# Six of the 42 low parts of each two-pass expert's weight tiles are made by GpSimd

## The chip, the cores and the metric

The kernel runs on one core of one Trainium2 chip. The metric is device time in microseconds (us) of one execution: 1571.8 us, the median of three runs (1571.66 to 1572.39). The engines are TensorE (PE; its weight loads are PEld), VectorE (DVE), ScalarE (ACT), GpSimd (POOL) and SyncE (SP), which issues the weight loads to the DMA engines.

## The reference

Two encoder layers over 256 tokens of width 1024, and a last RMSNorm. Layer 0 is a pooling mixer and a dense SwiGLU, layer 1 an attention mixer and a mixture of eight experts, of which each token takes two. The change lies in the experts:

```python
def _swiglu(h, w_gate_up, w_down):
    gu = h @ w_gate_up
    g, u = gu[..., :D_FF], gu[..., D_FF:]
    return (jax.nn.silu(g) * u) @ w_down

def _moe(h, router, w_gate_up, w_down):
    logits = (h @ router).astype(jnp.float32)
    top_v, top_i = lax.top_k(logits, TOP_K)
    gates = jax.nn.softmax(top_v, axis=-1)
    ...
    y = jnp.zeros_like(h)
    for e in range(N_EXPERTS):
        y = y + gate_full[..., e:e + 1] * _swiglu(h, w_gate_up[e], w_down[e])
    return y
```

D_FF is 3584. All weights are float32.

## The kernel before

**Numbers in two parts.** TensorE multiplies in a rounded float32 format. A weight tile (128 partitions x 2048, 1 MB) is therefore split into a high part, `whi` (ScalarE copies it into that format, `make_hi`, L314), and a low part, `wlo` = raw - high (VectorE subtracts, `make_lo`, L320). The tokens are split in the same way. A three-pass product adds high x high, high x low and low x high, 12 matmuls of 512 columns for a tile.

**Experts.** The experts are put in an order by how many tokens they have, and worked one after the other as items n = 0 to 7 (item n is also called expert n below). Each has 42 tiles: 28 of gate and up weights, in seven slabs of four (two gate tiles, which are summed in bank G, two up tiles in bank U), then 14 down tiles (banks Y0, Y1). Items with even n have up to 128 tokens and three passes (`full_item`). Items with odd n have up to 64 tokens, and the two parts of the tokens lie side by side in the 128 columns of TensorE, so that two passes do: 8 matmuls for a tile (`half_item`, L902, L903 in the gate stage, L939, L940 in the down stage). After each slab TensorE adds the two halves again with 16 small matmuls into bank T (`turn_slab`, L915), ScalarE and VectorE take the SiLU, the product `th` (L1768) and split it into `hTh` (ScalarE, and a small low part by VectorE, L1350).

**Rings and waits.** SP loads tile t into one of seven raw buffers (RAW = 7); the load of tile t waits until the low part of tile t-7 is made. `whi` and `wlo` have three buffers (CUT = 3): both parts of tile t wait until TensorE has used tile t-3 (`tile_used`). TensorE waits for the low part of a tile, which implies its high part. Every engine works its own written order, so one that waits holds up all that is behind it on that engine.

**GpSimd in the experts.** For each item it issues a gather of the next item's tokens (`e_tok`, L488), when their row numbers are there (`from_ready`, made by VectorE after slab 6 has begun), and at the item's end one or two scatter-adds of its result (L496). Before the last norm the sum is read back (L501).

Of the kernel before, what the change touches and what calls it, by code (L numbers as in the profile page):

```python
# [28 lines left out]
P = 128  # L29
RAW = 7  # L30
CUT = 3
# [10 lines left out]
E = 8  # L42
CAP = 128
HALF_CAP = 64
LOW = 4
# [6 lines left out]
ALU = mybir.AluOpType  # L52
ACT = mybir.ActivationFunctionType
F32 = mybir.dt.float32
# [11 lines left out]
FFN_TILES = DOWN + 2 * DT  # L66
T_ATT = T_FFN + FFN_TILES
HALF_TILES = 20
T_MOE = T_ATT + 2 * HALF_TILES
# [4 lines left out]
def count(i, per, plus=0):  # L74

    if isinstance(i, int):
        return i * per + plus
    register, step, first = i
    return register * (step * per) + (first * per + plus)


def one(i):
# [7 lines left out]
def encoder(nc, x_in, rel_bias, gains_t, norm_ffn, norm_final, a_w_in, a_w_group, a_scale, a_w_out,  # L90
            b_w_in, b_w_out, f_w_gate_up, f_w_down, m_router, m_w_gate_up, m_w_down,
            c_ident, c_pool, c_bucket, c_band, c_class, c_tri, c_iota, c_tab, c_dump, out):
    with ExitStack() as ctx:
        sem = lambda name: ctx.enter_context(nc.semaphore(name))
# [17 lines left out]
        raw = place("raw", [RAW, 2048], F32)  # L112
# [114 lines left out]
        spare_zero = sem("spare_zero")  # L227
        c_in = [sem(f"const{i}") for i in range(15)]
        raw_full = [sem(f"raw_full{i}") for i in range(RAW)]
        hi_done, lo_done, tile_used = sem("hi_done"), sem("lo_done"), sem("tile_used")  # L230
        chain = sem("chain")
        ms_done, std_done, hn_done = sem("ms_done"), sem("std_done"), sem("hn_done")
        rstd_done, x_sum, sq_done = sem("rstd_done"), sem("x_sum"), sem("sq_done")
# [76 lines left out]
        def make_hi(act, t, item=0):  # L310
# [2 lines left out]
                act.wait_ge(tile_used, count(item, FFN_TILES, t - CUT + 1))  # L313
            nc.scalar.activation(whi[:, t % CUT], raw[:, t % RAW], ACT.Copy).then_inc(hi_done, 1)  # L314

        def make_lo(dve, t, item=0):
            dve.wait_ge(hi_done, count(item, FFN_TILES, t + 1))
            if t >= CUT:
                dve.wait_ge(tile_used, count(item, FFN_TILES, t - CUT + 1))
            nc.vector.tensor_tensor(wlo[:, t % CUT], raw[:, t % RAW], whi[:, t % CUT].bitcast(F32),  # L320
                                    ALU.subtract).then_inc(lo_done, 1)
# [33 lines left out]
        def _(sp):  # L355
# [8 lines left out]
            def load(t, item=0, src=None, rows_together=False):  # L364

                if t >= RAW:
                    sp.wait_ge(lo_done, count(item, FFN_TILES, t - RAW + 1))
                if rows_together:
                    dst, src = raw[:, t % RAW], src.rearrange("(p b) n -> p (b n)", b=2)
                elif t == T_GROUP:  # L370
                    dst = raw[:, t % RAW].rearrange("p (b n) -> p b n", n=256)
                    src = a_w_group[0].rearrange("g (c p) n -> p (g c) n", p=P)
                else:
                    dst = raw[:, t % RAW].rearrange("p (k n) -> p k n", n=512)
                    src = (tile_source(t) if src is None else src).rearrange("(k p) n -> p k n", p=P)
                sp.dma_start(dst, src).then_inc(raw_full[t % RAW], 16)
# [67 lines left out]
        def _(pool):  # L444
# [36 lines left out]
                pool.dma_start(acc_dram[r * P:r * P + P, :], x[:, r % NT]).then_inc(acc_done, 16)  # L481

            pool.wait_ge(hn_out, 32)
            summed = 48
            for n in range(E - 1):
                pool.wait_ge(from_ready, n + 1)
                rows = slice(0, HALF_CAP if n % 2 == 0 else P)
                nc.gpsimd.indirect_dma_start(e_tok[rows], None, hn_dram,  # L488
                                             bass.IndirectOffsetOnAxis(from_rows[rows, 0:1], 0)).then_inc(e_full, 16)
                pool.wait_ge(slot_ready, n + 1)  # L490
                pool.wait_ge(y_hi, 2 * n + 2)
                width = P if n % 2 == 0 else HALF_CAP
                for first in range(0, P, width):
# [2 lines left out]
                    nc.gpsimd.indirect_dma_start(acc_dram, bass.IndirectOffsetOnAxis(to_rows[0:width, 0:1], 0), y_out[to],  # L496
                                                 None, compute_op=ALU.add).then_inc(acc_done, 16)
                    summed += 16
            pool.wait_ge(acc_done, summed)
            for tb in range(NT):  # L500
                pool.dma_start(x[:, tb], acc_dram[tb * P:tb * P + P, :]).then_inc(x_back, 16)  # L501

            pool.wait_ge(x_final, 1)
            pool.wait_ge(c_in[C_GAIN4], 16)
# [3 lines left out]
        @block.tensor  # L508
        def _(pe):
            def tile_ready(t, item=0):  # L510
                pe.wait_ge(lo_done, count(item, FFN_TILES, t + 1))

            def turn_x(n, kh):

# [1379 lines left out]
```

## Time and profile before

| | |
|---|---|
| median of three runs | 1571.8 us |
| profiled execution, its own time | 1573.2 us |
| its span, first to last instruction | 1571.3 us |
| PE busy | 1493.0 us, 95% |
| DVE busy | 1177.1 us, 75% |
| ACT busy | 1005.3 us, 64% |
| POOL busy | 131.9 us, 8% |
| low parts of weight tiles on DVE (L320) | 426 of 2298 ns, 974.9 us |
| high parts on ACT (L314) | 426 of 1912 ns, 812.0 us |
| granted TensorE clock, mean | 0.994 |
| experts in the span | from about 627 us on, item 3 from 985.5 to 1093 |

Shares of busy time are averages over stages with different limits; the experts take the last 940 us and there the odd and the even items differ. A busy TensorE is a TensorE with matmuls in its pipeline: of 512 columns each, they start 0.23 us apart and are shown with 0.40.

### The profile page before, as it was taken

How to read it: one execution, taken by the hardware profiler on the slowest of the kernel's cores; microseconds unless marked ns; L12 is line 12 of the kernel's file. 1: busy time of each engine (PE TensorE's matmuls, PEld its weight loads, DVE VectorE, ACT ScalarE, POOL GpSimd, SP SyncE). 2: the span in 40 equal slices, each digit the busy share in tenths (PEclk: the TensorE clock that was granted, in tenths of full speed). 3: DMA queues.
4: the chain of work that ended last, by engine and by line, in shares of the span. 5: the costliest groups of instructions: out<-in, count | busy, mean ns of one | idle time of the engine just before them, and what ended most of it. 6: DMA issues, size and time to landing. Idle time of an engine off the chain costs nothing.

```text
span 1571.3 us, 19731 instructions
## 1 busy us (share of the span) xinstructions
PE 1493.0 (95%) x7570; PEld 1214.4 (77%) x7570; DVE 1177.1 (75%) x1008; ACT 1005.3 (64%) x861; POOL 131.9 (8%) x130
## 2 busy tenths in 40 slices
PE   8999999999999999999998999999999999999985
PEld 6888888899879977778776888776787776787763
DVE  4555454464565566898899888999898999888996
ACT  5453443343453356677887776888776888777884
POOL 0000000022125031300000100000000000000000
PEclk9999999999999999999999999999999999999998
DMA  9655555566516731999999999999999999999994
GB/s 335 209 175 187 179 170 187 188 204 218 168 47 210 227 108 55 358 361 368 358 395 410 379 398 395 371 399 406 379 403 390 373 405 396 384 396 394 378 387 172
DMA packets 200275, 468.34 MB, mean 298 GB/s; under 512 B 9793, under 2 KB 15937, under 8 KB 187633
## 3 DMA queue, kind: packets, MB, share of 16 engines
q1 hardware_dynamic: 193872, 453.93, 79.5%
q0 software_dynamic: 2816, 9.96, 2.2%
q10 hardware_dynamic: 3488, 3.13, 0.6%
q8 instruction: 62, 1.02, 0.3%
q14 instruction: 37, 0.30, 0.1%
HBM read 459.62 MB, written 7.37 MB: 297 GB/s over the span
## 4 chain that ended last, share of the span: by engine, by line
PE 69%; DVE 11%; DMA 9%; ACT 6%; issue 3%; SPq 2%; DVEq 0%; ACTq 0%
DVE wlo L320 7%; DMA raw<-in_m_w_gate_up_dram 6%; PE bY L337 6%; PE bY L339 6%; PE bY L338 6%; ACT whi L314 5%; PE bG L337 4%; PE bG L339 4%; PE bG L338 4%; PE bU L337 4%; PE bU L339 4%; PE bU L338 4%; PE bS L339 3%; PE bS L337 3%; PE bS L338 3%
## 5 line engine op out<-in xcount | busy, mean ns | idle before, releaser
L320 DVE TENSOR_TENSOR wlo<-raw,whi 128x2048 fp32r<-128x2048 f32 x426 | 974.9, 2298 | 308.1 <-ACT whi L314 305.3
L314 ACT ACTIVATE whi<-raw 128x2048 fp32r<-128x2048 f32 x426 | 812.0, 1912 | 422.3 <-PE bS L339 132.9
L939 PE MATMUL bY<-whi,hTh 128*128 128x512 f32 x224 | 92.5, 413 | 16.9 <-DVE wlo L320 16.2
L902 PE MATMUL bG<-whi,eTh 128*128 128x512 f32 x224 | 92.0, 411 | 16.5 <-DVE wlo L320 16.5
L902 PE MATMUL bU<-whi,eTh 128*128 128x512 f32 x224 | 91.8, 410 | 5.7 <-DVE wlo L320 5.7
L337 PE MATMUL bG<-whi,eTh 128*128 128x512 f32 x224 | 90.3, 403 | 6.9 <-DVE wlo L320 3.6
L337 PE MATMUL bU<-whi,eTh 128*128 128x512 f32 x224 | 90.8, 406 | 0.0
L337 PE MATMUL bY<-whi,hTh 128*128 128x512 f32 x224 | 89.7, 400 | 0.0
L903 PE MATMUL bG<-wlo,eTh 128*128 128x512 f32 x224 | 89.0, 397 | 0.0
L940 PE MATMUL bY<-wlo,hTh 128*128 128x512 f32 x224 | 88.9, 397 | 0.0
L338 PE MATMUL bG<-whi,eTl 128*128 128x512 f32 x224 | 88.9, 397 | 0.0
L339 PE MATMUL bG<-wlo,eTh 128*128 128x512 f32 x224 | 88.9, 397 | 0.0
L338 PE MATMUL bY<-whi,hTl 128*128 128x512 f32 x224 | 88.9, 397 | 0.0
L339 PE MATMUL bY<-wlo,hTh 128*128 128x512 f32 x224 | 88.9, 397 | 0.0
L903 PE MATMUL bU<-wlo,eTh 128*128 128x512 f32 x224 | 88.9, 397 | 0.0
L339 PE MATMUL bU<-wlo,eTh 128*128 128x512 f32 x224 | 88.8, 397 | 0.0
L338 PE MATMUL bU<-whi,eTl 128*128 128x512 f32 x224 | 88.8, 396 | 0.0
L459 POOL TENSOR_TENSOR bias<-biasrev,band 128x256 f32<-128x256 f32 x32 | 36.4, 1137 | 510.8 <-DMA biasrev<-toeplitz 384.3
L939 PEld LDWEIGHTS bY<-whi,hTh 128*128 128x128 f32 x224 | 42.1, 188 | 40.3 <-issue 25.7
L902 PEld LDWEIGHTS bG<-whi,eTh 128*128 128x128 f32 x224 | 42.0, 188 | 39.7 <-DVE wlo L320 25.0
L337 PEld LDWEIGHTS bG<-whi,eTh 128*128 128x128 f32 x224 | 42.1, 188 | 22.2 <-DVE wlo L320 7.8
L902 PEld LDWEIGHTS bU<-whi,eTh 128*128 128x128 f32 x224 | 42.1, 188 | 18.1 <-DVE wlo L320 9.4
(439 smaller groups left out, 2923.3 us busy)
## 6 DMA issues: line engine op xcount, KB each, us to landing
raw<-in_m_w_gate_up_dram SPq DMA_DIRECT2D x224, 1024.0 KB, 12.3
raw<-in_m_w_down_dram SPq DMA_DIRECT2D x112, 1024.0 KB, 11.7
raw<-in_b_w_in_dram SPq DMA_DIRECT2D x36, 1024.0 KB, 5.2
raw<-in_f_w_gate_up_dram SPq DMA_DIRECT2D x28, 1024.0 KB, 5.2
raw<-in_f_w_down_dram SPq DMA_DIRECT2D x14, 1024.0 KB, 5.0
raw<-in_a_w_out_dram SPq DMA_DIRECT2D x4, 1024.0 KB, 16.1
biasrev<-toeplitz SPq DMA_DIRECT2D x32, 128.0 KB, 4.8
raw<-in_b_w_out_dram SPq DMA_DIRECT2D x4, 1024.0 KB, 5.1
```

Source lines behind the costliest of these rows:

```text
L314: nc.scalar.activation(whi[:, t % CUT], raw[:, t % RAW], ACT.Copy).then_inc(hi_done, 1)
L320: nc.vector.tensor_tensor(wlo[:, t % CUT], raw[:, t % RAW], whi[:, t % CUT].bitcast(F32), ALU.subtract).then_inc(lo_done, 1)
L337: pe.matmul(dst, a[0], b[0], start=start, stop=False)
L338: pe.matmul(dst, a[1], b[0], start=False, stop=False)
L339: return pe.matmul(dst, a[0], b[1], start=False, stop=stop)
L459: nc.gpsimd.tensor_tensor(to[:, 0:S].rearrange("p (a m) -> p a m", a=4), rev(0, 4), band[:, qt].rearrange("p (a m) -> p a m", a=4), ALU.add)
L902: pe.matmul(backward(bank, 0, 512), xs[:, kb], w[0], start=kb == 0, stop=False)
L903: mm = pe.matmul(backward(bank, 0, 512), xs[:, kb], w[1], start=False, stop=stop and b == len(ks) - 1)
L939: pe.matmul(to, hTh[:, kb], w[0], start=kb == 0, stop=False)
L940: mm = pe.matmul(to, hTh[:, kb], w[1], start=False, stop=stop)
```

## The change

In the odd items the low parts of tiles 6, 12, 18, 24, 29 and 34 are made by GpSimd, with the same subtraction. `by_pool` says which tiles these are. They count up a semaphore of their own, `lo_pool`; `lows` gives the count that a waiting engine needs on either semaphore, and `low_ready` waits for the right one: in TensorE before the tile's matmuls, and in SP before the load that reuses the tile's raw buffer. `make_lo` leaves these tiles out on VectorE. Nothing else is computed in another way.

```diff
--- before.py
+++ after.py
@@ -77,6 +77,33 @@
         return i * per + plus
     register, step, first = i
     return register * (step * per) + (first * per + plus)
+
+
+POOL_LOWS = (6, 12, 18, 24, 29, 34)
+
+
+def by_pool(t, n):
+
+    u = t - T_MOE
+    if not isinstance(n, int) or u < 0:
+        return False
+    n, u = n + u // FFN_TILES, u % FFN_TILES
+    return n % 2 == 1 and n < E and u in POOL_LOWS
+
+
+def lows(t, n):
+
+    if not isinstance(n, int):
+        return count(n, FFN_TILES, t + 1 - LOW * len(POOL_LOWS))
+    all_tiles = n * FFN_TILES + t + 1
+    u = all_tiles - 1 - T_MOE
+    if u < 0:
+        return all_tiles
+    n, u = divmod(u, FFN_TILES)
+    if by_pool(t=T_MOE + u, n=n):
+        return len(POOL_LOWS) * (n // 2) + POOL_LOWS.index(u) + 1
+    here = sum(p < u for p in POOL_LOWS) if n % 2 == 1 and n < E else 0
+    return all_tiles - len(POOL_LOWS) * (min(n, E) // 2) - here
 
 
 def one(i):
@@ -227,7 +254,7 @@
         spare_zero = sem("spare_zero")
         c_in = [sem(f"const{i}") for i in range(15)]
         raw_full = [sem(f"raw_full{i}") for i in range(RAW)]
-        hi_done, lo_done, tile_used = sem("hi_done"), sem("lo_done"), sem("tile_used")
+        hi_done, lo_done, lo_pool, tile_used = sem("hi_done"), sem("lo_done"), sem("lo_pool"), sem("tile_used")
         chain = sem("chain")
         ms_done, std_done, hn_done = sem("ms_done"), sem("std_done"), sem("hn_done")
         rstd_done, x_sum, sq_done = sem("rstd_done"), sem("x_sum"), sem("sq_done")
@@ -313,7 +340,18 @@
                 act.wait_ge(tile_used, count(item, FFN_TILES, t - CUT + 1))
             nc.scalar.activation(whi[:, t % CUT], raw[:, t % RAW], ACT.Copy).then_inc(hi_done, 1)
 
+        def low_ready(engine, t, item=0):
+            engine.wait_ge(lo_pool if by_pool(t, item) else lo_done, lows(t, item))
+
+        def make_lo_pool(pool, t, item):
+            pool.wait_ge(hi_done, item * FFN_TILES + t + 1)
+            pool.wait_ge(tile_used, item * FFN_TILES + t - CUT + 1)
+            nc.gpsimd.tensor_tensor(wlo[:, t % CUT], raw[:, t % RAW], whi[:, t % CUT].bitcast(F32),
+                                    ALU.subtract).then_inc(lo_pool, 1)
+
         def make_lo(dve, t, item=0):
+            if by_pool(t, item):
+                return
             dve.wait_ge(hi_done, count(item, FFN_TILES, t + 1))
             if t >= CUT:
                 dve.wait_ge(tile_used, count(item, FFN_TILES, t - CUT + 1))
@@ -364,7 +402,7 @@
             def load(t, item=0, src=None, rows_together=False):
 
                 if t >= RAW:
-                    sp.wait_ge(lo_done, count(item, FFN_TILES, t - RAW + 1))
+                    low_ready(sp, t - RAW, item)
                 if rows_together:
                     dst, src = raw[:, t % RAW], src.rearrange("(p b) n -> p (b n)", b=2)
                 elif t == T_GROUP:
@@ -481,12 +519,19 @@
                 pool.dma_start(acc_dram[r * P:r * P + P, :], x[:, r % NT]).then_inc(acc_done, 16)
 
             pool.wait_ge(hn_out, 32)
+            def lows_of(n, tiles):
+                if n % 2 == 1:
+                    for t in tiles:
+                        make_lo_pool(pool, T_MOE + t, n)
+
             summed = 48
             for n in range(E - 1):
+                lows_of(n, POOL_LOWS[:4])
+                rows = slice(0, HALF_CAP if n % 2 == 0 else P)
                 pool.wait_ge(from_ready, n + 1)
-                rows = slice(0, HALF_CAP if n % 2 == 0 else P)
                 nc.gpsimd.indirect_dma_start(e_tok[rows], None, hn_dram,
                                              bass.IndirectOffsetOnAxis(from_rows[rows, 0:1], 0)).then_inc(e_full, 16)
+                lows_of(n, POOL_LOWS[4:])
                 pool.wait_ge(slot_ready, n + 1)
                 pool.wait_ge(y_hi, 2 * n + 2)
                 width = P if n % 2 == 0 else HALF_CAP
@@ -496,9 +541,11 @@
                     nc.gpsimd.indirect_dma_start(acc_dram, bass.IndirectOffsetOnAxis(to_rows[0:width, 0:1], 0), y_out[to],
                                                  None, compute_op=ALU.add).then_inc(acc_done, 16)
                     summed += 16
+            lows_of(E - 1, POOL_LOWS[:2])
             pool.wait_ge(acc_done, summed)
             for tb in range(NT):
                 pool.dma_start(x[:, tb], acc_dram[tb * P:tb * P + P, :]).then_inc(x_back, 16)
+            lows_of(E - 1, POOL_LOWS[2:])
 
             pool.wait_ge(x_final, 1)
             pool.wait_ge(c_in[C_GAIN4], 16)
@@ -508,7 +555,7 @@
         @block.tensor
         def _(pe):
             def tile_ready(t, item=0):
-                pe.wait_ge(lo_done, count(item, FFN_TILES, t + 1))
+                low_ready(pe, t, item)
 
             def turn_x(n, kh):
```

The instructions of GpSimd from the gather in item 0 to the gather in item 2 (e_tok: the gathered tokens of the next item; summed: the scatter-adds), before:

```order
L488 DMA e_tok<-normed,from_rows 64x1024
L496 DMA summed<-y_out,to_rows 384x1024
L488 DMA e_tok<-normed,from_rows 128x1024
L496 DMA summed<-y_out,to_rows 384x1024 x2
L488 DMA e_tok<-normed,from_rows 64x1024
```

and in the changed kernel:

```order
L532 DMA e_tok<-normed,from_rows 64x1024
L541 DMA summed<-y_out,to_rows 384x1024
L349 TENSOR_TENSOR wlo<-raw,whi 128x2048 x4
L532 DMA e_tok<-normed,from_rows 128x1024
L349 TENSOR_TENSOR wlo<-raw,whi 128x2048 x2
L541 DMA summed<-y_out,to_rows 384x1024 x2
L532 DMA e_tok<-normed,from_rows 64x1024
```

Four lows stand ahead of the gather of item 1, and two between it and the scatter-adds. In item 7 two stand ahead of the read-back of the sum and four behind it.

VectorE in slabs 4 to 6 and the start of the down stage of item 3, from the low of tile 21 on (th: the product with the SiLU; hTh: the small low part of the hidden rows; from_rows: the row numbers for the gather), before:

```order
L320 TENSOR_TENSOR wlo<-raw,whi 128x2048 x2
L1350 TENSOR_TENSOR hTh<-th,hTh 128x4x64
L320 TENSOR_TENSOR wlo<-raw,whi 128x2048 x2
L1768 TENSOR_TENSOR th<-bT,tsilu 128x256
L320 TENSOR_TENSOR wlo<-raw,whi 128x2048 x2
L1350 TENSOR_TENSOR hTh<-th,hTh 128x4x64
L320 TENSOR_TENSOR wlo<-raw,whi 128x2048 x2
L1768 TENSOR_TENSOR th<-bT,tsilu 128x256
L1723 CAST from_rows<-bX 128x1
L320 TENSOR_TENSOR wlo<-raw,whi 128x2048 x2
L1350 TENSOR_TENSOR hTh<-th,hTh 128x4x64
L320 TENSOR_TENSOR wlo<-raw,whi 128x2048 x4
```

and in the changed kernel:

```order
L358 TENSOR_TENSOR wlo<-raw,whi 128x2048 x2
L1397 TENSOR_TENSOR hTh<-th,hTh 128x4x64
L358 TENSOR_TENSOR wlo<-raw,whi 128x2048
L1815 TENSOR_TENSOR th<-bT,tsilu 128x256
L358 TENSOR_TENSOR wlo<-raw,whi 128x2048 x2
L1397 TENSOR_TENSOR hTh<-th,hTh 128x4x64
L358 TENSOR_TENSOR wlo<-raw,whi 128x2048 x2
L1815 TENSOR_TENSOR th<-bT,tsilu 128x256
L1770 CAST from_rows<-bX 128x1
L358 TENSOR_TENSOR wlo<-raw,whi 128x2048
L1397 TENSOR_TENSOR hTh<-th,hTh 128x4x64
L358 TENSOR_TENSOR wlo<-raw,whi 128x2048 x3
```

The lows of tiles 24 and 29 are gone from their pairs; those of the other tiles stand in the same order between the same small operations.

## Rows read from the trace of the kernel before

**Rows 1.** Windows, columns: stretch and length, PE, PEld, DVE, ACT, POOL busy, clock, DMA, GB/s

```profile
863.50:985.50 122.00, 122.00 (x541) 98.17 (x540) 105.60 (x66) 88.68 (x61) 6.97 (x3) 1.00 1.04 390
985.50:1093.00 107.50, 97.62 (x461) 76.15 (x460) 100.58 (x66) 91.38 (x75) 2.88 (x2) 1.00 1.04 393
```

**Rows 2.** Waits of expert 3: who for whom, total us, times, longest

```profile
PE bG L902 <- DVE wlo L320: 4.2, 6, 1.3
...
ACT whi L314 <- DMA raw<-in_m_w_down_dram: 2.3, 4, 0.6
```

**Rows 3.** Waits of expert 1

```profile
ACT whi L314 <- DMA raw<-in_m_w_down_dram: 6.3, 9, 1.6
```

**Rows 4.** Waits of expert 7

```profile
ACT whi L314 <- DMA raw<-in_m_w_down_dram: 8.6, 13, 0.9
```

**Rows 5.** Chain of waits, a gate slab of expert 3: start us, us, what

```profile
1013.32 1.92 ACT whi L314
1015.26 2.30 DVE wlo L320
1017.61 0.50 PE bG L902
1019.74 1.82 PE bT L915 x16
...
1023.58 1.92 ACT whi L314
```

**Rows 6.** Timeline of ACT, the same slab: start, us, engine, line, operation

```profile
1010.01 1.90 ACT L314 ACTIVATE whi<-raw 128x2048 fp32r<-128x2048 f32 x1
...
1015.93 3.71 ACT L314 ACTIVATE whi<-raw 128x2048 fp32r<-128x2048 f32 x2
```

**Rows 7.** Timeline of DVE, the same slab

```profile
1010.11 4.49 DVE L320 TENSOR_TENSOR wlo<-raw,whi 128x2048 fp32r<-128x2048 f32 x2
...
1020.07 0.42 DVE L1350 TENSOR_TENSOR hTh<-th,hTh 128x256 fp32r<-128x256 f32 x1
```

**Rows 8.** Timeline of POOL, bias additions of the attention

```profile
344.89 0.52 POOL L462 TENSOR_TENSOR bias<-biasrev,classes 128x128 f32<-128x128 f32 x1
...
347.17 0.85 POOL L459 TENSOR_TENSOR bias<-biasrev,band 128x256 f32<-128x256 f32 x1
347.99 2.56 POOL L462 TENSOR_TENSOR bias<-biasrev,classes 128x128 f32<-128x128 f32 x1
```

**Rows 9.** Timeline of DVE at the same time

```profile
347.19 2.98 DVE L320 TENSOR_TENSOR wlo<-raw,whi 128x2048 fp32r<-128x2048 f32 x1 [0.59 <-ACT whi L314]
```

**Rows 10.** Timeline of POOL, the last norm

```profile
1559.87 2.35 POOL L505 TENSOR_TENSOR hn<-x,gain 128x1024 f32<-128x1024 f32 x1 [100.36 <-DVE x L1829]
```

**Rows 11.** Timeline of DVE, the square alone and at the last norm

```profile
22.83 1.22 DVE L1340 CUSTOM_DVE_ANT_0 hn<-x 128x1024 f32<-128x1024 f32 x1
...
1560.48 2.83 DVE L1340 CUSTOM_DVE_ANT_0 squares<-x 128x1024 f32<-128x1024 f32 x1
```

**Rows 12.** Timeline of POOL, a multiplication before the experts

```profile
625.80 6.94 POOL L476 TENSOR_SCALAR hn<-hn,small 128x1024 f32<-128x1024 f32 x1 [8.81 <-DVE hnl L1559]
```

**Rows 13.** Timeline of DVE at the same time

```profile
625.52 4.49 DVE L320 TENSOR_TENSOR wlo<-raw,whi 128x2048 fp32r<-128x2048 f32 x2
```

**Rows 14.** Timeline of POOL, the gathers in experts 3 and 5

```profile
1057.22 1.00 POOL L488 DMA_INDIRECT e_tok<-normed,from_rows  x1 [66.23 <-DVE from_rows L1723]
...
1287.24 3.02 POOL L488 DMA_INDIRECT e_tok<-normed,from_rows  x1 [66.33 <-DVE from_rows L1723]
```

**Rows 15.** Timeline of PE, start of tile 29 in expert 3

```profile
1059.69 0.47 PE L939 MATMUL bY<-whi,hTh 128*128 128x512 f32 x1 [0.79 <-DVE wlo L320]
```

**Rows 16.** Chain of waits, end of expert 3's down stage

```profile
1074.79 12.43 DMA raw<-in_m_w_gate_up_dram
...
1091.39 0.74 DVE eTl L1350 x2
```

## The prediction

> **What bounds the kernel now.** I read the windows first, one for each expert. In a window row the columns are the stretch, its length, then the busy time of TensorE (PE), its weight loads, VectorE (DVE), ScalarE (ACT) and GpSimd (POOL), and the clock. A three-pass expert (n even) keeps TensorE busy for all of its window; a two-pass expert (n odd: 1, 3, 5, 7) does not: TensorE is busy 97.6 of 107.5 us, VectorE 100.6, ScalarE 91.4, GpSimd 2.9 [rows 1]. So TensorE's tile time sets the even experts, and nothing that the change touches stands there. In the odd ones three engines are nearly full and GpSimd is empty, which invites the change; whether it pays depends on which wait ends last.
>
> The waits of expert 3 say it: TensorE waits 4.2 us in six places for a low part in the gate stage, and ScalarE waits 2.3 us for weights from DMA in the down stage [rows 2]. The chain of waits shows the loop behind those six places. In the slab at 1013 us it goes: TensorE ends a tile, ScalarE makes the high part of the tile three further on (1.92), VectorE its low part (2.30), TensorE multiplies it, turns the hidden rows (1.82 for 16 matmuls), multiplies the next tile, and is back at the same place 10.26 us later, 1013.32 to 1023.58 [rows 5]. Every link waits for the one before it, because only three cut tiles exist. Such a loop has no slack: a delay put into it isn't made good in the next slab. VectorE is in the loop for 2.3 of 10.3 us; the rest of its work lies beside it. This is a latency loop, not a VectorE queue.
>
> **The change, part by part.** Removed from VectorE: 6 lows in each of 4 experts, 24 x 2.3 [rows 5] = 55 us of busy time. Added on GpSimd: 24 subtractions of 128x2048. The trace of before has none of that size. The nearest row is 128x1024 of the same operation, 2.35 us [rows 10]; twice that is 4.7 us; with the 0.52 us of a 128x128 one [rows 8] as the start of a line, 0.52 + 1920 x (2.35 - 0.52) / 896 gives 4.44. I take 4.5. A GpSimd tensor_scalar of 128x1024 took 6.94 us [rows 12], of which 4.2 were waiting behind VectorE (below), so 2.7 for half the size: 5.4 is my upper end, 4.4 my lower. A price that only a page has: the Trainium skill, "GPSIMD Engine Reference", section 3.1, gives 4497 ns for this very shape against 2293 ns on VectorE; with it the sum below would be the same.
>
> The second part of the price is whether the two engines work side by side. They do not. At 347.19 VectorE began a low part while GpSimd was in an addition begun at 347.17; the low took 2.98 us, 0.7 more than the usual 2.3, which is the rest of GpSimd's 0.85; and GpSimd's next one, issued at 347.99 behind it, took 2.56 us where its like takes 0.52 [rows 8, 9]. At the end of the span a VectorE square of 128x1024, 1.22 us when alone, took 2.83 beside GpSimd's 2.35 us multiplication: 1560.48 + 1.61 is 1562.1, where GpSimd ended [rows 10, 11]. So either waits for the whole instruction of the other. The Trainium skill, "SBUF — State Buffer", says the same of the shared port pair: an exclusive lock held for the whole instruction by whichever starts first, also by a VectorE operation with two SBUF inputs. By that rule the trace agrees.
>
> A low moved to GpSimd thus holds the pair for 4.5 us in place of 2.3 and frees nothing for the lows behind it. As plain work: 36 x 2.25 + 6 x 4.5 + 7 small lows of 0.42 [rows 7] = 111 us of the pair in an expert of 107.5 us, so at least +3 each, +12 in all. That is the floor. The loop makes it more:
>
> - Tiles 12 and 24 (the first of a slab). Tile 12 itself is in [rows 6, 7]. Its high part ends at 1011.9, VectorE is in tile 11's low until 1012.4 (the first of the two in 4.49), GpSimd then works until 1016.9. TensorE left tile 10 at 1013.3 and needs about 1.9 for tile 11, so it reaches tile 12 at 1015.2 and waits. VectorE's low of tile 13, on the loop at 1015.26 [rows 5], can't start before 1016.9: +1.6 us.
> - Tiles 6 and 18 (the third of a slab; tile 14 stands for them). The high part is ready at 1017.8 [rows 6], VectorE's low of 13 ends at 1017.6 and a small low behind it at 1018.0; GpSimd 1018.0 to 1022.5. TensorE is free for the tile at 1021.6 (1019.74 + 1.82 [rows 5]): it waits 0.9. Behind GpSimd, VectorE owes the lows of 15, 16 and 17: they run 1022.5 to 1029.6 with a small multiply between, where the loop before had 17's low at 1025.5 to 1027.8 (one period after 1015.26). +1.8 us.
> - Gate stage: 2 x 1.6 + 2 x 1.8 = 6.8 us.
> - Tile 29. On GpSimd's queue it stands behind the gather e_tok, whose issue takes 1.00 us in expert 3, begun at 1057.22 [rows 14]. So GpSimd works from 1058.3 to 1062.8, and TensorE, which started the tile at 1059.69 [rows 15], starts it at 1062.9: +3.2. Queued behind it on GpSimd are only the scatter-adds of the expert's end.
> - Tile 34. GpSimd puts 4.5 in the place of 2.3, and VectorE's next low waits behind it: +2.2, together 5.4.
> - The loads. SP's load of tile t+7 now waits for GpSimd's low, and all later loads wait behind it on SP's queue. Seven tiles at 10.26 / 4 = 2.6 us are 18 us, a load lands in 12.4 [rows 16]; less the 2 to 3 us by which the high part goes first, some 3 us are in hand, about what the low comes later: no term. The gather behind the first four lows comes some 10 us after tile 24's low is due and isn't held.
> - Given back: before, from 1074.79 the chain ran through a DMA of 12.43 us [rows 16], so VectorE had spare time: from the end of tile 35's low (1074.6) the seven lows to the next expert's first need 7 x 2.25 = 15.8 us, to 1090.4, and the chain shows 1091.39 there [rows 16]. With the loads no longer late, 1.0 to 1.2 us comes back. Down stage: 5.4 - 1.2 = 4.2.
>
> Expert 3: 6.8 + 4.2 = 11. Expert 5 has the same, but its gather takes 3.02 us to issue [rows 14]: 2 more, 13. Expert 1 waits 6.3 us for down weights [rows 3] where expert 3 waits 2.3; half of that difference is hidden waiting that a slower expert doesn't repeat: 11 - 2 = 9. Expert 7 waits 8.6 [rows 4]: 3 less, and no gather stands before tile 29, 1 less: 7. Sum 9 + 11 + 13 + 7 = 40 us. The even experts start later and take as long. The profiled execution lasted 1573.2 us (span 1571.3 and 1.9 around it), 1.4 above the median of 1571.8: 1571.8 + 40 = 1612.
>
> **The rivals.**
>
> - Passed over (slower still). When GpSimd asked at 625.80, VectorE had two lows queued, 4.49 us together, and GpSimd got in only after both [rows 12, 13]: the one that waits is not next. If a low of tile t+1 is ready whenever GpSimd wants the pair for tile t, TensorE stands another 2.25 us at t, and has t+1 ready after, so loses about 1.9 more. In the loop VectorE has nothing ready then (13's high part comes 2.8 us after 12's lock could be had), so only the few late places count. All 24 tiles would give +45, 1657; half of them 1634.
> - Side by side (a smaller loss). If 4.5 us operations did overlap with the lows, tiles 12 and 24 would end at 1016.4 against TensorE's 1015.2 and 0.7 would remain on the loop, 6 and 18 would cost 0.9, the down stage some 1.5: 4.7 for an expert, 3 in experts 1 and 7, +16, 1588. The stretched rows [rows 9, 11] speak against it.
> - Faster. The place is the down stage, and the gate tile of each slab where TensorE waits for VectorE; the freed 55 us would let those lows start earlier. It needs no lock and a GpSimd low that ends within TensorE's lead, 3.3 us after the high part (1011.9 to 1015.2). Then at most the 4.2 us of waiting in [rows 2] goes in each expert, 17 in all, and rather half of it: 1564. Against it: 2.35 us for half a tile already breaks the 3.3.
> - No change: delays and DMA slack cancel. All waits of ScalarE for DMA in an odd expert are 2.3 to 8.6 us, less than the 11 lost in all of them.
>
> **How the numbers follow.** Forecast with the lock, about 1612: 0.70. Passed over: 0.10. Side by side: 0.11. Faster: 0.05. No change: 0.04. A difference under 0.2%, 3 us, can't be told from none with this kernel. For the range: the operation at 4.4 or 5.4 us moves the sum by -2 or +22; a loop that forgives half of each delay goes down towards the floor of 1584. From 1588 (side by side) to 1636 (half passed over, or the 5.4) holds eight in ten. Faster 0.05, same 0.04, slower 0.91.
>
> **What the profile after should show.** GpSimd's subtraction at 4.5 us or a little above, 24 of them, more where it begins during a low; VectorE's lows no longer all 2.29 but some of 3 to 5 us, with starts before GpSimd's end; the window of expert 3 some 118 us and the even ones as before; new waits of TensorE for GpSimd's wlo, some 1 to 3 us each; ScalarE's waits for DMA nearly gone. I'm wrong if the lows stay at 2.29 us beside a busy GpSimd, or if TensorE's waits at those six tiles are made good before the expert ends.

## The result and the profile after

The changed kernel takes 1612.24 us (median, 1610.82 to 1614.61) against 1571.76 for the kernel before: 40.5 us more, ratio 1.0258 with a 95% interval of 1.024 to 1.0276. Ratios leave out executions in the slower state of the chip: of all runs these are two of the ten of e_free below (1642.8 and 2060.1 us at a clock of 0.85 and 0.65), without which its median is 1569.1.

From its page, busy time of the engines and the groups of the low parts (line, engine, operation, tiles and shapes, count, then busy us, mean ns of one, and the idle time before them with its releaser):

```profile
PE 1505.9 (94%) x7570; PEld 1222.2 (76%) x7570; DVE 1172.1 (73%) x984; ACT 1004.7 (62%) x861; POOL 244.0 (15%) x154
...
L358 DVE TENSOR_TENSOR wlo<-raw,whi 128x2048 fp32r<-128x2048 f32 x402 | 969.8, 2425 | 352.0 <-ACT whi L341 348.8
...
L349 POOL TENSOR_TENSOR wlo<-raw,whi 128x2048 fp32r<-128x2048 f32 x24 | 110.8, 4617 | 227.6 <-ACT whi L341 227.6
```

GpSimd has its 24 subtractions of 4.6 us. VectorE makes 24 lows fewer and is yet busy for 1172 us, 5 less than before: 24 x 2.298 = 55 us went, and 402 x (2.425 - 2.298) = 51 us came back, as lows that last longer. The median low still takes 2.29 us, and the few behind GpSimd carry it all (up to 4.98).

The windows of expert 3 and of expert 4 behind it (stretch and length, busy PE, PEld, DVE, ACT, POOL, granted clock, DMA share, GB/s):

```profile
994.50:1112.00 117.50, 99.84 (x456) 76.14 (x455) 98.31 (x59) 91.47 (x75) 30.39 (x8) 0.99 1.00 369
1112.00:1235.00 123.00, 123.00 (x547) 99.25 (x547) 106.82 (x67) 89.07 (x61) 7.46 (x3) 1.00 1.03 380
```

Expert 3 has become 10 us longer; the three-pass expert took 122.0 before [rows 1] and takes 123.0 in this window, whose ends are read only roughly. The scatter-adds at the experts' ends give it exactly. The timeline of GpSimd around expert 3:

```profile
997.55 1.88 POOL L541 DMA_INDIRECT summed<-y_out,to_rows  x1 [42.14 <-issue]
1005.65 4.55 POOL L349 TENSOR_TENSOR wlo<-raw,whi 128x2048 fp32r<-128x2048 f32 x1 [6.22 <-ACT whi L341]
1021.80 4.77 POOL L349 TENSOR_TENSOR wlo<-raw,whi 128x2048 fp32r<-128x2048 f32 x1 [11.59 <-ACT whi L341]
1039.34 4.55 POOL L349 TENSOR_TENSOR wlo<-raw,whi 128x2048 fp32r<-128x2048 f32 x1 [12.77 <-ACT whi L341]
1056.52 4.54 POOL L349 TENSOR_TENSOR wlo<-raw,whi 128x2048 fp32r<-128x2048 f32 x1 [12.62 <-ACT whi L341]
1070.84 0.99 POOL L532 DMA_INDIRECT e_tok<-normed,from_rows  x1 [9.78 <-DVE from_rows L1770]
1071.85 4.53 POOL L349 TENSOR_TENSOR wlo<-raw,whi 128x2048 fp32r<-128x2048 f32 x1
1088.12 4.57 POOL L349 TENSOR_TENSOR wlo<-raw,whi 128x2048 fp32r<-128x2048 f32 x1 [11.74 <-ACT whi L341]
1115.33 2.73 POOL L541 DMA_INDIRECT summed<-y_out,to_rows  x1 [22.63 <-issue]
```

From 997.55 to 1115.33 are 117.8 us; before, the same two adds stood at 989.12 and 1096.74, 107.6 apart. Taken like this, the odd experts grew by 9.9, 10.2, 14.3 and 4.0 us (1, 3, 5, 7; the last up to the last norm's multiplication) and the even ones behind them by 0.4 to 0.5.

What the lock does is seen at tile 6. The timeline of VectorE, two lows, the first cut out of its group by a narrow window:

```profile
1007.52 4.83 DVE L358 TENSOR_TENSOR wlo<-raw,whi 128x2048 fp32r<-128x2048 f32 x1 [2.09 <-ACT whi L341]
```

```profile
1025.07 3.65 DVE L358 TENSOR_TENSOR wlo<-raw,whi 128x2048 fp32r<-128x2048 f32 x1 [2.58 <-ACT whi L341]
```

GpSimd subtracts from 1005.65 to 1010.20. VectorE's next low is issued at 1007.52 and takes 4.83 us: 2.54 of waiting, until 1010.06, and its own 2.29. The other one meets tile 12's, 1021.80 to 1026.57: 3.65 us, of which 1.36 are waiting. These answer to the 2.98 of [rows 9].

TensorE's waits in expert 3 (engine, tile and line, releaser: total us, times, longest):

```profile
PE bY L986 <- POOL wlo L349: 5.9, 2, 3.6
...
PE bG L949 <- POOL wlo L349: 3.2, 2, 1.8
PE bG L949 <- DVE wlo L358: 2.9, 6, 1.4
...
PE bU L949 <- POOL wlo L349: 1.8, 2, 0.9
```

In [rows 2] TensorE waited 4.2 us for VectorE in the gate stage; now it waits 2.9 there for VectorE, and 10.9 in both stages for GpSimd, 3.6 of it in one piece at tile 29. No wait for DMA is left in this expert.

**What was not foreseen** is in the windows of 2 us around tile 29, here with the granted clock as the third number from the end:

```profile
1074.00:1076.00 2.00, 0.00 (x0) 0.00 (x0) 2.00 (x1) 1.56 (x1) 2.00 (x1) 1.00 1.04 436
1076.00:1078.00 2.00, 1.47 (x5) 1.27 (x6) 2.00 (x1) 0.00 (x0) 0.38 (x1) 0.83 1.08 369
1078.00:1080.00 2.00, 2.00 (x8) 1.61 (x7) 2.00 (x3) 0.30 (x1) 0.00 (x0) 0.50 0.83 322
1080.00:1082.00 2.00, 2.00 (x15) 2.00 (x15) 1.44 (x2) 1.61 (x1) 0.00 (x0) 0.81 0.86 303
```

TensorE stands still until 1076.5, and when it starts again its clock falls from 2.4 to 1.2 GHz and stays there for some 3.4 us. The changed kernel has seven such stretches in its odd experts, one of them double, some 27 us in all: at 835, 852, 1077, 1268, 1319, 1337 and 1575 us. The kernel before has none in the experts. Not every stop is followed by one. The three stops at tile 29 (3.6 to 3.8 us) all were; of the four at tile 34 (2.3 us) three were, expert 3's was not; of the five in gate stages (1.8 to 1.9 us, at tile 12 and in expert 7 also at tile 24) only one was, at tile 12 of expert 5.

### The profile page after: what moved, and what is told of

Same layout as the page of the kernel before. It is cut to its first block and busy times, and to the rows that moved or that the text cites. A ratio compares the mean times of both kernels' runs of the same rounds, so it can differ in the third digit from the quotient of the medians.

```text
span 1609.0 us, 19731 instructions
## 1 busy us (share of the span) xinstructions
PE 1505.9 (94%) x7570; PEld 1222.2 (76%) x7570; DVE 1172.1 (73%) x984; ACT 1004.7 (62%) x861; POOL 244.0 (15%) x154
## 5 line engine op out<-in xcount | busy, mean ns | idle before, releaser
L349 POOL TENSOR_TENSOR wlo<-raw,whi 128x2048 fp32r<-128x2048 f32 x24 | 110.8, 4617 | 227.6 <-ACT whi L341 227.6
L986 PE MATMUL bY<-whi,hTh 128*128 128x512 f32 x224 | 96.8, 432 | 27.4 <-POOL wlo L349 21.6
L987 PE MATMUL bY<-wlo,hTh 128*128 128x512 f32 x224 | 94.0, 420 | 0.0
L375 PE MATMUL bY<-whi,hTh 128*128 128x512 f32 x224 | 89.7, 400 | 0.0
L377 PE MATMUL bY<-wlo,hTh 128*128 128x512 f32 x224 | 88.9, 397 | 0.0
L949 PEld LDWEIGHTS bG<-whi,eTh 128*128 128x128 f32 x224 | 42.6, 190 | 50.9 <-issue 24.5
```

The costliest lines, as they stand in the source:

```text
L349: nc.gpsimd.tensor_tensor(wlo[:, t % CUT], raw[:, t % RAW], whi[:, t % CUT].bitcast(F32), ALU.subtract).then_inc(lo_pool, 1)
L375: pe.matmul(dst, a[0], b[0], start=start, stop=False)
L377: return pe.matmul(dst, a[0], b[1], start=False, stop=stop)
L949: pe.matmul(backward(bank, 0, 512), xs[:, kb], w[0], start=kb == 0, stop=False)
L986: pe.matmul(to, hTh[:, kb], w[0], start=kb == 0, stop=False)
L987: mm = pe.matmul(to, hTh[:, kb], w[1], start=False, stop=stop)
```

## The experiments

The code is shortened to what differs, and calls are cut short in it. The kernel before was run beside them each time, at 1570.1 to 1571.8 us. The table below has the medians and, from the profiles, the steps between the gate copies of ScalarE in expert 3, which mark the slabs. Tile 6 lies in the step from slab 1 to 2, tile 12 in 2 to 3, tile 18 in 4 to 5, tile 24 in 5 to 6, and tiles 29 and 34 in the last column, from slab 6 to the next expert's first slab. For example, in the changed kernel the copies stand at 1007.66, 1019.32, 1030.95, 1041.22.

| kernel | median us | to before | slab 1-2 | 2-3 | 3-4 | 4-5 | 5-6 | down stage |
|---|---|---|---|---|---|---|---|---|
| before | 1571.8 | | 10.29 | 10.27 | 10.27 | 10.90 | 10.52 | 46.63 |
| changed | 1612.2 | +40.5 | 11.66 | 11.63 | 10.27 | 12.83 | 11.39 | 52.30 |
| e_gate | 1587.4 | +15.7 | 11.68 | 12.95 | 10.27 | 12.81 | 11.41 | 46.19 |
| e_down | 1593.8 | +22.1 | 10.30 | 10.26 | 10.30 | 10.90 | 10.49 | 56.15 |
| e_spare | 1603.5 | +31.8 | 11.68 | 11.69 | 10.29 | 12.82 | 11.44 | 50.79 |
| e_dual | 1678.5 | +106.9 | 14.60 | 15.43 | 10.26 | 15.25 | 15.09 | 55.38 |
| e_one | 1645.2 | +74.9 | 13.98 | 14.47 | 10.28 | 14.32 | 13.99 | 53.74 |
| e_write | 1570.6 | +0.5 | 10.29 | 10.27 | 10.28 | 10.90 | 10.49 | 47.15 |
| e_latency | 1584.7 | +14.6 | 10.50 | 10.30 | 10.29 | 10.87 | 10.50 | 49.03 |
| e_late46 | 1593.6 | +23.3 | 11.41 | 11.26 | 10.28 | 11.54 | 11.26 | 50.55 |
| e_split | 1582.1 | +11.8 | 10.76 | 11.00 | 10.29 | 12.00 | 10.49 | 48.49 |
| e_free | 1569.6 | -0.7 | 10.30 | 10.29 | 10.27 | 10.53 | 10.50 | 47.43 |
| e_halves | 1572.8 | +2.8 | 10.11 | 10.19 | 10.10 | 11.25 | 10.33 | 46.54 |
| e_both | 1573.1 | +2.4 | 10.10 | 9.79 | 10.20 | 10.60 | 10.33 | 50.05 |

**e_gate and e_down: the two parts alone.**

```diff
-POOL_LOWS = (6, 12, 18, 24, 29, 34)
+POOL_LOWS = (6, 12, 18, 24)        # e_gate; e_down: (29, 34)
```

> One part alone: GpSimd makes the lows of the gate-stage tiles 6, 12, 18 and 24 of the odd experts; tiles 29 and 34 go back to VectorE. In the profile of the changed kernel the slabs with these tiles grew by 1.37, 1.36, 1.93 and 0.87 us in expert 3. Theory A (shared port pair plus the latency loop): the same growth stays, 5.5 us in experts 1, 3 and 5 and 3.5 in expert 7, less up to 1.2 us each that the down stage gives back from waits for DMA: 1572 + 20 - 4 = 1588. Theory B (the loss comes mostly from TensorE's clock, which fell to 1.2 GHz seven times in the odd experts of the changed kernel, six of them in the down stage): almost nothing is left, below 1580.

> The other part alone: GpSimd makes tiles 29 and 34 only. Theory A: the rest of the 40 us, some 4.2 us in experts 1 and 3, 8 in expert 5 (where the clock fell three times) and little in expert 7, less what the DMA waits in an odd expert that has not been slowed before don't allow to hide: 1572 + 18 to 22 = 1592. Theory B: 1600 or more, with nearly all the falls of the clock.

Measured: ratios 1.0100 (1.0080 to 1.0121) and 1.0139 (1.0119 to 1.0158). Theory A's numbers are met, 1588 and 1592 forecast, 1587.4 and 1593.8 measured; the two parts together make 37.8 of the 40.5. That is in part chance, because theory A had no term for the clock, and it fell more often here. e_gate has a slab of 12.95 us in expert 3 where the changed kernel has 11.63: TensorE's stop of 1.8 us at tile 12, followed by a fall in one expert of the changed kernel, was followed by one in all four here. Each of these stretches of 3.4 us at 1.2 GHz thus cost some 1.3 us. e_down's down stage is 3.9 us longer than the changed kernel's, with four times 3.4 us at 1.2 GHz in place of one. Its profile took 1599.6 us, 6 above its median, so its row in the table is on the long side.

**e_spare: the clock held.** In TensorE's program, ahead of the wait for a low of GpSimd:

```diff
+                if by_pool(t, item):
+                    spare(SPARES[u], eTh[:, 0], eTh[:, 0:4])
                 low_ready(pe, t, item)
+SPARES = {6: 3, 12: 6, 18: 3, 24: 6, 29: 12, 34: 8}
```

> The changed kernel, and TensorE fills its wait for each of GpSimd's lows with matmuls whose result nobody reads (3 for tiles 6 and 18, 6 for 12 and 24, 12 for 29, 8 for 34; 0.23 us each), to keep its clock at 2.4 GHz. The changed kernel had 23.9 us at 1.2 GHz in the experts; if the matmuls there were on the path, the clock is worth up to 12 us: 1601 (theory B and a mixed one). Theory A alone, with VectorE, ScalarE and GpSimd setting the pace while TensorE waits: 1612, whatever the clock does. If the spare matmuls last longer than the waits, a little is lost.

Measured: 1603.5, ratio 1.0215 (1.0192 to 1.0238), 8.7 us less than the changed kernel. Its windows at the same place:

```profile
1076.00:1078.00 2.00, 2.00 (x16) 1.82 (x15) 2.00 (x3) 0.94 (x1) 0.00 (x0) 1.00 0.90 315
1078.00:1080.00 2.00, 2.00 (x13) 1.77 (x13) 2.00 (x2) 0.98 (x1) 0.00 (x0) 1.00 0.84 305
```

There is no stretch at 1.2 GHz left in its experts (the expectation gave the changed kernel's stretches as 23.9 us, since it counted the double one once). The clock was worth 8.7 us, the rest of the loss is 31.8. The two intervals leave some 3 us of doubt on each of these (30.2 to 37.4 us for this kernel's loss, 37.7 to 43.4 for the changed one's). It also sorts out expert 5: there the down stage is 50.9 us as in the others, where the changed kernel had 54.9; the extra 4 us of that expert were the clock.

**e_dual, e_write and e_one: who shares what.** All lows on VectorE; at the same 24 places and behind the same waits GpSimd does something for which nobody waits:

```diff
+            nc.gpsimd.tensor_tensor(xTl, hnh, hnl, ALU.subtract)              # e_dual: reads two
+            nc.gpsimd.memset(xTl, 0.0); nc.gpsimd.memset(xTl, 0.0)            # e_write: reads none
+            nc.gpsimd.tensor_scalar(xTl, hnh, 1.0, None, ALU.mult)            # e_one: reads one
```

> VectorE makes all 42 lows as in the kernel before; GpSimd makes, at the same 24 places and with the same waits, one more subtraction of 128x2048 from two tensors in SBUF that nobody waits for, into a tensor nobody reads. Nothing waits for GpSimd, so only the sharing of the ports can cost. Lock theory: each of the 24 holds VectorE up for nearly its 4.5 us, because the tile's own low is due at that moment: up to 24 x 3.9 = 94 us, less what is slack: 1640 to 1665. Side by side theory: 1572. If the waiting instruction is passed over while VectorE has lows queued, GpSimd's operations are shown with 7 us and more.

> As the run with one more subtraction on GpSimd (e_dual), but in the place of each subtraction two memsets of 128x2048, which read nothing in SBUF; in the kernel before a memset of 128x1024 took 0.95 us, so some 4 us for the two. Nobody waits for them. If the pair is shared only where GpSimd reads SBUF: 1572. If any GpSimd operation of that length holds VectorE's lows up: 24 x 3 us and more, above 1630.

> As e_dual (all lows on VectorE, something more on GpSimd at the same 24 places, nobody waits for it), but the GpSimd operation has one input in SBUF, a multiplication of 128x2048 by a constant. If only two-input operations of GpSimd take the pair: 1572. If any GpSimd operation that reads SBUF does, it holds VectorE's lows up for its length each time; the 2.7 us that a 128x1024 one of this kind took before the experts would make 5 us: 1670 or more, and if it takes 2 to 3 us, 1610 to 1640.

Measured: 1678.5 (ratio 1.0685, 1.0665 to 1.0705), 1570.6 (1.0000, 0.9989 to 1.0011) and 1645.2 (1.0479, 1.0462 to 1.0497). The low parts on VectorE (count, then ns shortest/median/longest) and GpSimd's own operation, first in e_dual:

```profile
L328 DVE TENSOR_TENSOR wlo<-raw,whi x426: 2274/2291/6644, 16.6 to 1655.6; 128x2048 fp32r<-128x2048 f32 x142
```

```profile
L321 POOL TENSOR_TENSOR xTl<-hnh,hnl x24: 4739/6645/6668, 764.4 to 1633.9; 128x2048 fp32r<-128x2048 f32 x24
```

then in e_write, the 312 lows from 698 us on, where GpSimd's memsets stand among them:

```profile
L328 DVE TENSOR_TENSOR wlo<-raw,whi x312: 2280/2292/2352, 698.0 to 1549.3; 128x2048 fp32r<-128x2048 f32 x156
```

and in e_one:

```profile
L321 POOL TENSOR_SCALAR xTl<-hnh x24: 5392/7464/7527, 763.0 to 1601.8; 128x2048 fp32r<-128x2048 f32 x24
```

A subtraction for which nobody waits costs 107 us, more than the change itself and some 13 above the range given for the lock, and two memsets cost nothing. Not all of it is waiting for the pair: in the experts the clock stood at 1.2 GHz for 112 us in e_dual and 72 in e_one, which at the 1.3 us for 3.4 us that e_gate shows makes some 43 and 27 us, an estimate. So the price is in reading SBUF on GpSimd beside VectorE's lows, which have two inputs there (no run has a one-input operation of VectorE in their place). One input on GpSimd is enough for it; e_one's 1645 lies between its two ranges, its operation taking longer than the 5 us guessed and costing less. The runs also show who gets the pair. In e_dual most of GpSimd's 24 took 6.65 us, which is 4.5 and 2.1 of one low; in e_one 7.47, which is 5.4 and 2.1. GpSimd waits for the rest of one low and is then let in. This holds with a second low ready. The timeline of e_dual in expert 3, tile 6:

```profile
1022.12 3.88 ACT L314 ACTIVATE whi<-raw 128x2048 fp32r<-128x2048 f32 x2
1024.06 8.85 DVE L328 TENSOR_TENSOR wlo<-raw,whi 128x2048 fp32r<-128x2048 f32 x2 [0.17 <-ACT whi L314]
1024.11 6.65 POOL L321 TENSOR_TENSOR xTl<-hnh,hnl 128x2048 fp32r<-128x2048 f32 x1 [6.22 <-ACT whi L314]
```

The next tile's high part is ready at 1026.0, before the low under way ends at 1026.35, and still GpSimd's subtraction goes first: the second low ends only at 1032.9. VectorE's longest low, 6.64, is 4.35 of waiting and 2.29 of its own: it was issued just when GpSimd got in, and GpSimd came first. So the rival of the passed over instruction is refuted for the lows, and in the changed kernel the longest of the 24 is 5.0 us. Why the multiplication before the experts took 6.94 us beside two lows [rows 12, 13] stays unexplained. The one behind it fits the lock no better. In the kernel before:

```profile
632.73 4.86 POOL L476 TENSOR_SCALAR hn<-hn,small 128x1024 f32<-128x1024 f32 x1
```

```profile
635.81 2.29 DVE L320 TENSOR_TENSOR wlo<-raw,whi 128x2048 fp32r<-128x2048 f32 x1 [0.93 <-ACT whi L314]
```

This low begins while GpSimd multiplies, until 637.59, and yet takes its ordinary 2.29 us. The changed kernel and e_dual show the same there. So the exclusion is shown for the operations of these runs, not for every one of GpSimd that reads SBUF.

**e_latency and e_late46: late tiles without the lock.** VectorE makes all lows; TensorE waits, for the six tiles, also for GpSimd's memsets, 3.7 us of them in the first, 4.7 in the second, which also has the spare matmuls:

```diff
+                    pe.wait_ge(lo_pool, ...)      # the last memset for this tile
                 pe.wait_ge(lo_done, count(item, FFN_TILES, t + 1))
```

> As e_write, and TensorE waits, for tiles 6, 12, 18, 24, 29 and 34 of the odd experts, for both: VectorE's low part and the end of GpSimd's two memsets (about 4 us from the moment the high part is ready). So the tile comes as late as GpSimd can bring it, while VectorE works on undisturbed: the side by side case. Theory A (lock plus loop) takes the lateness of the tile itself as the smaller part: TensorE is 0.8 us late at tiles 12 and 24, 0.3 at 6 and 18, 2.6 at 29, most of which the loop takes over: 3 to 4 us an expert, 1582 to 1588. A theory in which the lateness of the six tiles is all and the ports matter little expects some 1600, the changed kernel with its clock held.

> As e_latency, with three memsets on GpSimd that last 4.6 us together (two of 2048 columns, one of 1024), as long as the subtraction they stand for, and the spare matmuls of e_spare ahead of TensorE's wait, so that the clock holds. It is the changed kernel with its clock held (1603.5) less the sharing of the ports: the six tiles come as late, but VectorE isn't held up. Theory A (the lock costs beyond the lateness): TensorE is late by 1.3 us at 12 and 24 and 0.8 at 6 and 18, half of which the loop takes over since the lows behind are ready, and 3 us in the down stage: 1586 to 1592. If lateness explains all of it: 1603.

Measured: 1584.7 (1.0096, 1.0070 to 1.0121), in theory A's range, and 1593.6 (1.0146, 1.0129 to 1.0163), 2 us above its range and 10 below the other one's. GpSimd in e_late46, expert 3, tiles 6 and 12, and VectorE's lows from 698 us on:

```profile
1003.47 4.69 POOL L322 MEMSET xTl<- 128x2048 f32 x3 [6.19 <-ACT whi L314]
1019.36 4.69 POOL L322 MEMSET xTl<- 128x2048 f32 x3 [11.21 <-ACT whi L314]
```

```profile
L328 DVE TENSOR_TENSOR wlo<-raw,whi x312: 2277/2292/2294, 698.1 to 1573.1; 128x2048 fp32r<-128x2048 f32 x156
```

No low is held up there, and the slabs still grow by 1.1, 1.0, 0.6 and 0.7 us, where the changed kernel with its clock held has 1.4, 1.4, 1.9 and 0.9. In the down stage the two are equal, 50.55 and 50.79. So lateness of the tile alone is 23.3 us of the 31.8, and the shared ports 8.5, nearly all in the gate stage; with the two intervals the 8.5 is uncertain by some 5 us. (In e_late46 VectorE still makes the 24 lows; e_free below shows that this relief is worth nothing where no tile is late.) The step between 3.7 and 4.7 us tells how steep it is: with 3.7 a slab grows by 0.0 to 0.2 us, with 4.7 by 0.6 to 1.1. (e_latency has no spare matmuls, and its clock fell twice in the experts, in none of these slabs.) TensorE comes to the tile 3.3 to 3.8 us after its high part (tile 12: 1011.9 to 1015.2, tile 14: 1017.8 to 1021.6, from the times that the prediction worked with). What fits into it is free, and of the one microsecond by which 4.7 exceeds 3.7 the slabs pay 0.7 to 1.0.

**e_split: half of each low on GpSimd.**

```diff
-            nc.gpsimd.tensor_tensor(wlo[:, t % CUT], ...)
+            nc.gpsimd.tensor_tensor(wlo[:, t % CUT, 0:1024], ...)      # VectorE the columns 1024 to 2047
```

> For the six tiles GpSimd makes the first 1024 columns of the low part and VectorE the other 1024; TensorE and SP wait for both; spare matmuls ahead of TensorE's wait (2, 3, 2, 3, 6, 4). If the engines worked side by side the tile would be ready 2.4 us after its high part, as before, and VectorE would be relieved of 24 x 1.1 us: 1572 or a little less. By the lock the two halves come one after the other, 2.35 + 1.2 us in place of 2.3, about half of what the whole tile costs: 1586 to 1590.

Measured: 1582.1, ratio 1.0076 (1.0059 to 1.0093). A loss of 11.8, some 4 us less than the 1586 to 1590 forecast from late halves and the lock, and far from a gain. Slab 5-6 costs nothing, slab 4-5 1.1 us.

**e_free: what an offload could give at best.**

```diff
-            nc.vector.tensor_tensor(wlo[:, t % CUT], raw[:, t % RAW], whi[:, t % CUT].bitcast(F32),
+            cols = slice(0, 8 if odd else 2048)       # odd: one of the 24 lows
+            nc.vector.tensor_tensor(wlo[:, t % CUT, cols], raw[:, t % RAW, cols], whi[:, t % CUT, cols].bitcast(F32),
```

> The kernel before, but for the 24 tiles VectorE subtracts 8 columns in place of 2048 (the rest of the low part is left out, and old values stand there). It gives VectorE what a cost-free offload would give. If the loop and the DMA engines set the odd experts, VectorE's 52 us are worth almost nothing: 1566 to 1571. If VectorE's load were the bound as its 94% of an odd expert's window suggests, up to 50 us: 1520 to 1545.

Measured: 1569.6, ratio 0.9995 (0.9984 to 1.0005). The windows of expert 3:

```profile
985.50:1093.00 107.50, 98.09 (x463) 76.56 (x462) 89.00 (x66) 91.31 (x74) 2.60 (x3) 1.00 1.04 393
```

VectorE is busy for 89.0 us in place of 100.6 [rows 1], and the expert is not a microsecond shorter. TensorE's waits in it have stayed too, 3.8 us in six places where [rows 2] have 4.2:

```profile
PE bG L904 <- DVE wlo L322: 3.8, 6, 0.9
```

This is the plainest answer to the idea of the change: in this kernel the load taken off VectorE is worth nothing at any price of its new home.

**e_halves and e_both: the loop made shorter.** For tiles 5, 9, ... 33 ScalarE and VectorE work in halves; e_both also leaves out six lows.

```diff
+                nc.scalar.activation(whi[:, t % CUT, 0:1024], raw[:, t % RAW, 0:1024], ACT.Copy).then_inc(hi_half, 1)
+                nc.scalar.activation(whi[:, t % CUT, 1024:2048], raw[:, t % RAW, 1024:2048], ACT.Copy).then_inc(hi_done, 1)
...
+                dve.wait_ge(hi_half, halves(t, item))
```

> The kernel before, all lows on VectorE, but for tiles 5, 9, 13, 17, 21, 25, 29 and 33 of the odd experts ScalarE makes the high part in two halves of 1024 columns and VectorE starts on the first half's low when that is there. If the odd experts are set by the loop ScalarE, VectorE, TensorE (10.26 us for a slab, 4.2 of it the two cuts), the loop gets 0.75 us shorter, until VectorE's own work (9.8 us and 0.1 for the split) takes over: 0.3 to 0.4 us for each of 28 slabs and a little in the down stage, 1572 - 11 = 1561. If VectorE's load sets them, it gets slower by the fixed cost of 32 more instructions: 1574 to 1576.

> The two that gave nothing alone, together: high and low parts in halves for tiles 5, 9, ... 33 (e_halves), and 8 columns in place of 2048 for six other lows of each odd expert (6, 12, 18, 24, 30, 34; the rest of these lows is left out, as in e_free). In e_halves VectorE had no gap left in a slab of 9.8 us, and the next one took 10.5. If VectorE's load is what stands right behind the loop, the slabs with a missing low fall to 9.8 us or less and the whole to 1560 to 1565. If a second loop or the DMA engines stand there, 1568 to 1572, and VectorE's load has no value in this kernel even then.

Measured: 1572.8 (1.0018, 1.0006 to 1.0029) and 1573.1 (1.0014, 1.0005 to 1.0023). My forecast of 1561 for e_halves was wrong. The slabs did get shorter, by 0.1 to 0.2 us instead of 0.3 to 0.4, in e_both down to 9.79, but the slab with the routing work got 0.35 longer, and what the gate stage of e_both won came back, and more, in its down stage (in expert 3 with a fall of the clock at 1089.5). The timeline of ScalarE there, high parts with the idle time before them:

```profile
1073.12 1.92 ACT L330 ACTIVATE whi<-raw 128x2048 fp32r<-128x2048 f32 x1 [0.58 <-DMA raw<-in_m_w_down_dram]
1075.60 1.91 ACT L330 ACTIVATE whi<-raw 128x2048 fp32r<-128x2048 f32 x1 [0.57 <-DMA raw<-in_m_w_down_dram]
1078.10 1.92 ACT L330 ACTIVATE whi<-raw 128x2048 fp32r<-128x2048 f32 x1 [0.58 <-DMA raw<-in_m_w_down_dram]
1080.60 1.92 ACT L330 ACTIVATE whi<-raw 128x2048 fp32r<-128x2048 f32 x1 [0.59 <-DMA raw<-in_m_w_down_dram]
1084.41 1.91 ACT L330 ACTIVATE whi<-raw 128x2048 fp32r<-128x2048 f32 x1 [1.90 <-DMA raw<-in_m_w_gate_up_dram]
```

Each waits for its weights: 1 MB every 2.49 us. So in the down stage the DMA engines stand behind the loop; at this pace the 42 tiles of an expert take 105 us, an estimate, of its 107.5. In the gate stage of e_both ScalarE doesn't wait for DMA, so what stands there is not shown. No version was found that beats the kernel before.

## Why the prediction was right, and where its terms were off

The time, 1612, the direction and the mechanism (the lateness of GpSimd's low in the loop of three cut tiles, and the exclusive ports) held. That the number agreed to 0.3 us is luck: terms of some 8 us too much and one of 8.7 us not foreseen stand against each other.

- GpSimd's price, 4.5 us forecast, 4.52 to 4.59 where it had the ports at once: right. The line through two sizes [rows 8, 10] had given 4.44.
- The exclusive use, read from stretched rows of other operations [rows 8 to 11]: right for the lows, and shown by e_dual against e_write. [Rows 12] were a poor witness for it: the 4.2 us of waiting in them, and with them the 2.7 us of work and the upper end of 5.4 us, are not shown, since the next multiplication ran beside a low. The share of the ports was over-rated. I called 12 us of port work the floor and wrote "The loop makes it more"; e_late46 shows the reverse order, 23.3 us from lateness and 8.5 from the ports. The rival of side by side work was priced at +16; with memsets of 4.7 us in GpSimd's place it is +23.3, since my 0.7 and 0.9 us for a gate tile measured 0.6 to 1.1 and a down stage, written as 1.5, is 3.9 (50.55 - 46.63).
- Gate stage, 6.8 us forecast for expert 3: 5.6 with the clock held (1.4, 1.4, 1.9 and 0.9 against 1.8, 1.6, 1.8 and 1.6). The step that was mis-sized is tile 24, priced like tile 12. It lies behind the slab with the routing work, which is longer already (10.90 before against 10.27); that the slack there came from this is only argued.
- Down stage, 4.2 forecast: 50.79 - 46.63 = 4.2 with the clock held. Right.
- Expert 5's gather of 3.02 us [rows 14] didn't come back; it took 1.01 us. The 2 us for it are void, and that expert 5 grew by 14.3 us, near my 13, had another cause: the clock fell three times there, once for twice as long. With the clock held the four experts grew by 7.8, 8.8, 9.0 and 4.2 us, where 9, 11, 13 and 7 were forecast.
- Expert 7, forecast 7, grew by 4.0. Its slabs already waited for DMA (11.04 us for slab 3-4 before, 10.18 after), so the loads hide more there than the 3 us I gave.
- The loads as no term: right. SP's later loads delayed nothing, and the median landing of the gate and up tiles fell from 12.3 to 8.9 us.
- The clock was no term at all in the forecast, and cost 8.7 us. I had looked at the gaps in the kernel before, where the clock held, and not asked what a stop of 3.6 us would do.
- The faster rival had a wrong upper end: 17 us were never to be had, as e_free shows. Most of the 4.2 us of waiting for VectorE in [rows 2] was waiting for the loop, not for VectorE's queue: 3.8 are left in e_free.

Open: why the multiplications before the experts don't fit the lock, which link sets the slabs of e_halves at 10.1 us, and what of the 11.8 us of e_split is lateness and what the ports.

## What to carry to other kernels

Before work is moved off an engine that is 94% busy, leave that work out for once and time it: here that showed 0 us to be had. An operation moved to a slower engine is free only if its whole length fits into the lead of its reader, here 3.3 to 3.8 us in the gate stage and some 2.5 at tile 34 (a low of 4.6 us there left TensorE a stop of 2.3), and a subtraction on GpSimd beside VectorE's takes the time of both. A wait of TensorE of some 2 to 4 us can cost more than itself, because its clock may fall behind it.

## What the runs showed of the hardware

- GpSimd's subtraction of two SBUF tensors and its multiplication of one by a constant, on 128x2048, and VectorE's float32 subtraction of two SBUF tensors exclude each other for whole instructions (lows of up to 6.64 us in e_dual, 5.74 in e_one, against 2.29). Memsets on GpSimd don't (e_write, 1.0000, lows of at most 2.35 us beside them). A multiplication of 128x1024 in the kernel before, at 632.73, overlaps a low of 2.29 us; this exception is open.
- In the experts the engine that waits was let in after the one instruction under way, in both directions: 6.65 = 4.5 + 2.1 us for GpSimd, also ahead of a low that was ready; 6.64 = 4.35 + 2.29 for VectorE. [Rows 12] don't fit this.
- A GpSimd multiplication of 128x2048 float32 by a constant takes 5.4 us (e_one, shortest), more than the two-input subtraction's 4.5.
- TensorE's granted clock went to 1.2 GHz for 3.4 us or twice that after stops of 1.8 to 3.8 us, in the changed kernel behind seven of twelve such stops; matmuls whose result nobody reads, put into the stops, took all of these away and gave 8.7 us.
